# Products of constants put into TensorE's waits in the second block's scan and latent up-projection

## The chip, the cores and the metric

The kernel runs on one core of a Trainium2 chip. The metric is the device time of one execution in microseconds (us); smaller is better. Its engines are named as in the profile: PE (TensorE, matrix products), PEld (its weight loads), DVE (VectorE), ACT (ScalarE), POOL (GpSimd) and SP (SyncE, which issues most DMAs). TensorE's clock has two levels, 1.2 and 2.4 GHz; the profile gives the granted clock as a share of 2.4 GHz, so 0.50 is the lower level and 1.00 the upper.

## The reference

Six transformer layers on 512 tokens of width 1024: four of a first block (two with forgetting attention, one S5, one pooling) and two of a second block, whose mixer is cut here to what the change touches:

```python
def hybrid_mixer(h, ...):
    proj = h @ w_in
    q_a, kv_a, k_pe, z, xbc, dt_raw = split(proj)
    q = (rmsnorm(q_a) @ w_q_up).reshape(b, s, MLA_HEADS, QK_HEAD_DIM)        # 8 heads of 64 + 32
    kv = (rmsnorm(kv_a) @ w_kv_up).reshape(b, s, MLA_HEADS, 64 + 64)
    # q_nope, q_pe, k_nope, k_pe are normalised, the pe parts rotated
    attn_out = causal_attention(q_full, k_full, v)
    # xbc goes through a convolution and silu, and gives xs, bm, cm
    y = ssd_chunked(xs, dt, a, bm, cm) + d_skip * xs                         # 4 chunks of 128 tokens, 8 heads
    yg = rmsnorm(y * silu(z)) * ssd_norm_w
    return concatenate([attn_out, yg]) @ w_out
```

## The kernel before, in words

The program is a list of stages that run one after the other (`plan`). Most stages form a Block of their own; a Block ends when all engines are at its end. Within a stage each engine has its own hand-written order (`tensor`, `scalar`, `gpsimd`, `vector`, `sync`), and engines wait for one another by semaphores (`e.wait_ge`, `then_inc`). TensorE's instructions are issued in the order written, so an instruction that is added stands ahead of everything behind it. SP loads the weights two slots ahead, under `chunk_done`.

A mixer of the second block is the stages `SecondIn`, `Ssd`, `LatentUp`, `LatentAttention` and `SplitProject`; it occurs twice, about 706 us apart.

`Ssd` (from L2488): TensorE multiplies B by C per chunk (L2522), turns B (L2526), x (L2530) and the rows of dt (L2536), and spreads the last row of the cumulated decays (L2540). ACT takes two exponentials of it (L2602, L2604). DVE scales the turned x (L2663, four instructions, semaphore `xdt_ready`; the last of them reads PSUM bank 7) and then scales these by the decays (L2667, three instructions, `xdtd_ready`). With those TensorE makes the states of three chunks (L2548, in banks 2 and 3), and DVE chains them (L2672 to L2676). Then a loop over 8 heads: `spread(h)` (L2560 to L2562, in banks 0/1 or 6/7), two exponentials on ACT (L2610, L2615), products by the cached C B on DVE (L2688) and POOL (L2634), and `out(h)` on TensorE (L2576, L2578). `spread(h + 1)` is issued ahead of `out(h)`. At the end four squares (L2621) are summed by TensorE (L2588), ACT takes two roots (L2624), DVE takes their reciprocals (L2696) and normalises (L2698).

`LatentUp` (from L2708): POOL packs the query weights (L2835, L2836, `packed`). TensorE makes ten raw tiles (L2765, L2770, L2772) and between them sums squares of the earlier ones in bank 6 (L2753, `stats`), and then four products for v (L2781). ACT takes the root (L2814), DVE the reciprocal (L2848), ACT and DVE split it in two (L2819, L2850, `stat_ready`). Then TensorE spreads the 11 statistics (L2800, banks 0 to 3, the next four ahead of DVE) and rotates three tiles (L2793, banks 4 and 5), DVE multiplies (L2872, L2879) and adds (L2855, L2861, L2865), and POOL does the cosines (L2839).

`LatentAttention` (L1978) follows: logits (L2018, L2019), maximum on DVE (L1948), exponential on ACT (L1900), scaling on POOL (L1918), turns on TensorE (L1796) and the product by v (L1809). ACT and DVE also split the first chunk of the output weights there (L1196, L1203).

`keep_warm(bank, n)` (L291) is in the kernel already: n products of two constants, `identb` by `pastb`, 128x512 in bf16, into a bank that nobody reads. All of its instructions have line L294. It is called in the norms, at the end of the projections and in three other stages, but nowhere in `Ssd`, `LatentUp` or `LatentAttention`.

Of the kernel before, what the change touches and what calls it, by code (L numbers as in the profile page):

```python
# [25 lines left out]
ST = S // P  # L26
# [55 lines left out]
def due(n):  # L82

    return not isinstance(n, int) or n > 0
# [248 lines left out]
class Stage:  # L333
    n = 0
# [10 lines left out]
    def tensor(self, e): pass  # L345
# [293 lines left out]
class PoolMix(Stage):  # L639

    n = 1
# [86 lines left out]
class S5Mix(Stage):  # L728


    n = 4
# [897 lines left out]
class FoxV(Split):  # L1629


    n = 4
# [94 lines left out]
class FoxAttention(Split):  # L1727


    n = FH // 2  # L1730
# [247 lines left out]
class LatentAttention(FoxAttention):  # L1978


    n = 0
# [40 lines left out]
class SplitProject(Split):  # L2022


    n = 4
# [191 lines left out]
class SplitGlu(Split):  # L2217


    n = DK  # L2220
# [102 lines left out]
class SecondIn(Split):  # L2323


    n = 8
# [161 lines left out]
class Ssd(Stage):  # L2488
# [24 lines left out]
    def tensor(self, e):  # L2513
        m, nc = self.m, self.m.nc
        ident = m.c("ident")
        tr, mm = nc.tensor.transpose, nc.tensor.matmul
        ps = m.ps

        for g in range(2):
            for c in range(ST):  # L2520
                cs = slice(c * P, (c + 1) * P)
                last = mm(ps[:, g, cs], self.bT(g)[:, cs], self.cT(g)[:, cs], start=True, stop=True)  # L2522
            last.then_inc(m.sem["cb_done"], 1)
        for g in range(2):
            for c in range(ST):
                last = tr(ps[:, 2 + g, c * P:(c + 1) * P], self.bT(g)[:, c * P:(c + 1) * P], ident)  # L2526
            last.then_inc(m.sem["bt_done"], 1)
        for c in range(ST):
            for t in range(4):
                last = tr(ps[:, 4 + c, t * P:(t + 1) * P], self.xs(t)[:, c * P:(c + 1) * P], ident)  # L2530
            last.then_inc(m.sem["xt_done"], 1)
        e.wait_ge(m.sem["acs_ready"], m.at("acs_ready", 1))
        e.wait_ge(m.sem["cb_ready"], m.at("cb_ready", 1))
        for i, src in enumerate((self.dt, self.acs)):
            for c in range(ST):
                last = tr(ps[:, 0, 32 * i + 8 * c:32 * i + 8 * c + 8], src[0:MH, c * P:(c + 1) * P], ident[0:MH, 0:MH])  # L2536
        last.then_inc(m.sem["rows_turned"], 1)
        e.wait_ge(m.sem["acsT_ready"], m.at("acsT_ready", 1))
        e.wait_ge(m.sem["cb_ready"], m.at("cb_ready", 2))
        mm(ps[:, 1, 0:32], m.c("last"), self.acsT, start=True, stop=True).then_inc(m.sem["last_spread"], 1)  # L2540

        for c in range(ST - 1):
            e.wait_ge(m.sem["xdtd_ready"], m.at("xdtd_ready", c + 1))
            e.wait_ge(m.sem["bt_ready2"], m.at("bt_ready2", 2))
            if due(c - 1):
                e.wait_ge(m.sem["st_ready"], m.at("st_ready", c - 1))
            for g in range(2):
                last = mm(ps[:, 2 + c % 2, g * 256:(g + 1) * 256], self.btok[:, g, c, :], self.xdtd[c][:, g * 256:(g + 1) * 256], start=True, stop=True)  # L2548
            last.then_inc(m.sem["st_done"], 1)

        def spread(h):
            b = 6 if h % 2 else 0
            e.wait_ge(m.sem["am_ready"], m.at("am_ready", h + 1))
            if h == 0:
                e.wait_ge(m.sem["decay_ready"], m.at("decay_ready", 1))
            if h == 1:
                e.wait_ge(m.sem["xdt_ready"], m.at("xdt_ready", ST))
            if due(h - 1):
                e.wait_ge(m.sem["l_ready"], m.at("l_ready", h - 1))
            mm(ps[:, b, :], m.ones[0:MH, :], self.am[h % 2][0:MH], start=True, stop=True).then_inc(m.sem["bc_ready"], 1)  # L2560
            mm(ps[:, b + 1, :], m.ones[32:MR, :], self.am[h % 2][32:MR], start=True, stop=False)
            mm(ps[:, b + 1, :], m.identb[:], m.pastb[:].rearrange("p (a n) -> p a n", a=1).broadcast_to([P, ST, P]), start=False, stop=True).then_inc(m.sem["bm_ready"], 1)  # L2562

        def out(h):
            bank = 4 + (h // 2) % 2
            e.wait_ge(m.sem["sc_ready"], m.at("sc_ready", h + 1))
            e.wait_ge(m.sem["cth_ready"], m.at("cth_ready", h + 1))
            e.wait_ge(m.sem["st_ready"], m.at("st_ready", ST - 1))
            if h == 0:
                e.wait_ge(m.sem["xdt_ready"], m.at("xdt_ready", ST))  # L2570
            if due(h // 2 - 1):
                e.wait_ge(m.sem["y_gated"], m.at("y_gated", h // 2 - 1))
            r = 64 * (h % 2)
            for c in range(ST):
                cs, hs = slice(c * P, (c + 1) * P), slice(h * 64, (h + 1) * 64)
                last = mm(ps[r:r + 64, bank, cs], self.xdt[c][:, hs], self.sc[h % 2][:, cs], start=True, stop=c == 0)  # L2576
                if c:
                    last = mm(ps[r:r + 64, bank, cs], self.st[c][:, hs], self.cth[h % 2][:, cs], start=False, stop=True)  # L2578
            last.then_inc(m.sem["yh_done"], 1)

        spread(0)
        for h in range(MH):
            if h + 1 < MH:
                spread(h + 1)
            out(h)
        for t in range(4):
            e.wait_ge(m.sem["ysq_ready"], m.at("ysq_ready", t + 1))
            last = mm(ps[:, 2 + t // 2, :], m.ones[:], m.sq[:, t % 2, :], start=t % 2 == 0, stop=t % 2 == 1)  # L2588
            last.then_inc(m.sem["ysq_used"], 1)

    def scalar(self, e):
        m, nc = self.m, self.m.nc
# [115 lines left out]
class LatentUp(Stage):  # L2708


    n = 2
# [33 lines left out]
    def tensor(self, e):  # L2745
        m, nc = self.m, self.m.nc
        mm, ps = nc.tensor.matmul, m.ps
        nope, pe = (self.packed[:, a:b].rearrange("p (k n) -> p k n", k=2) for a, b in ((0, 1024), (1024, 1536)))
        wk, wv = (m.w[(self.c0 + 1) % 2][:, 512 * i:512 * i + 512] for i in range(2))

        def stats(n):
            e.wait_ge(m.sem["isq_ready"], m.at("isq_ready", n + 1))
            mm(ps[0:32, 6, :], self.gather(n), self.square(n), start=n == 0, stop=n == self.N - 1).then_inc(m.sem["isq_used"], 1)  # L2753

        for n in range(1, self.N):
            if n == 1 or n == 3:
                e.wait_ge(m.sem["packed"], m.at("packed", 1 + n // 3))
            if n == 4:
                self.landed(e, 1, (self.c0 + 1) % 2)
            if n >= 5:  # L2760
                e.wait_ge(m.sem["raw_taken"], m.at("raw_taken", n - 4))
            out = ps[:, n % 4, :]
            if n < 3:
                for k in range(2):
                    last = mm(out, pe[:, k, P * n - P:P * n], m.lat[:, k, :], start=k == 0, stop=k == 1)  # L2765
            else:
                i = (n - 3) // 2
                if n % 2:
                    for k in range(2):
                        last = mm(out, nope[:, k, P * i:P * i + P], m.lat[:, k, :], start=k == 0, stop=k == 1)  # L2770
                else:
                    last = mm(out, wk[:, P * i:P * i + P], m.lat[:, 2, :], start=True, stop=True)  # L2772
            last.then_inc(m.sem["raw_ready"], 1)
            if n >= 3:
                stats(n - 3)
        for n in range(self.N - 3, self.N):
            stats(n)
        for t in range(ST):
            if t >= 2:
                e.wait_ge(m.sem["lv_taken"], m.at("lv_taken", t - 1))  # L2780
            last = mm(ps[:, 4 + t % 2, :], m.lat[:, 2, t * P:(t + 1) * P], wv, start=True, stop=True)  # L2781
            if t < ST - 1:
                last.then_inc(m.sem["lv_done"], 1)
        last.then_inc(m.chunk_done, 2)
        e.wait_ge(m.sem["stat_ready"], m.at("stat_ready", 1))

        def rotate(i):
            e.wait_ge(m.sem["normed"], m.at("normed", i + 1))
            if i == 0:
                e.wait_ge(m.sem["lv_taken"], m.at("lv_taken", ST))  # L2790
            if i == 2:
                e.wait_ge(m.sem["rot_taken"], m.at("rot_taken", 1))
            mm(ps[:, 4 + i % 2, :], m.c("rot"), self.pe[i], start=True, stop=True).then_inc(m.sem["rot_done"], 1)  # L2793

        for n in range(self.N):
            if n < 4:
                e.wait_ge(m.sem["raw_taken"], m.at("raw_taken", self.N - 1))
            else:
                e.wait_ge(m.sem["normed"], m.at("normed", n - 3))
            mm(ps[:, n % 4, :], m.spread[:, n * P:(n + 1) * P], m.stat2[0:64, :], start=True, stop=True).then_inc(m.sem["stat_spread"], 1)  # L2800
            if 3 <= n < 6:
                rotate(n - 3)

    def scalar(self, e):
        m, nc = self.m, self.m.nc
# [289 lines left out]
```

## Time and profile before

| | |
|---|---|
| median of 3 runs | 3875.01 us (3874.47 to 3875.34) |
| the profiled execution's own time | 3879.85 us |
| its span, from first to last instruction | 3878.0 us |
| mean granted TensorE clock | 0.969 |
| PE busy | 3611.3 us, 93% of the span, 16819 products |
| DVE, POOL, ACT busy | 53%, 28%, 28% |
| HBM traffic | 89 GB/s over the span |

The rows come from the profiled execution, so a sum made of them is made against 3879.85 us. Times in a timeline are microseconds from the start of the span; a row merges neighbouring instructions of one line ("x4"), its second number is how long they took in all, and the square bracket is the engine's idle time ahead of it and who ended it.

### The profile page before, as it was taken

The page shows a single profiled execution, that of the slowest core. Times are in us where ns is not written, and L with a number is a line of the kernel's source. Part 1 is how long each engine was busy: PE and PEld are TensorE (multiplying, and loading weights), DVE is VectorE, ACT ScalarE, POOL GpSimd, SP SyncE. Part 2 cuts the span into 40 slices and gives each one's busy share as a digit, 9 for nine tenths or more (in the row PEclk, how much of TensorE's full clock was granted, in tenths as well). Part 3 has the DMA queues.
Part 4 walks back from the last instruction along what each step waited for, and adds up shares of the span by engine and source line. Part 5 has one row for each costly group of instructions (what it writes and reads, how often), then busy time and mean ns, then how long its engine had stood idle before and what let it go on. Part 6 is the DMA issues. An engine that isn't in the chain of part 4 may idle for free. (4 is left out here: it accounts for less than half of the span.)

```text
span 3878.0 us, 44362 instructions
## 1 busy us (share of the span) xinstructions
PE 3611.3 (93%) x16819; PEld 2825.1 (73%) x16819; DVE 2053.9 (53%) x2627; ACT 1078.7 (28%) x1480; POOL 1100.2 (28%) x835
## 2 busy tenths in 40 slices
PE   7999999979999979999899999986899999689999
PEld 6767888757788858887667888762688877267887
DVE  4556556784544475455456545665533356654334
ACT  3542221131312122223452121333322223332121
POOL 0645543700645236340554634012100000130000
PEclk9999999989999989999999999997999999899999
DMA  3215443123444334442214443200133331013332
GB/s 106 61 49 131 128 132 98 52 69 94 136 129 133 90 87 135 126 115 80 66 41 116 131 130 107 80 25 22 55 102 99 87 88 47 22 44 87 92 99 80
DMA packets 554575, 346.08 MB, mean 89 GB/s; under 512 B 33526, under 2 KB 535676, under 8 KB 554428
## 3 DMA queue, kind: packets, MB, share of 16 engines
q1 hardware_dynamic: 540604, 293.80, 27.0%
q0 software_dynamic: 13824, 50.34, 4.5%
q8 instruction: 91, 1.49, 0.2%
q14 instruction: 56, 0.46, 0.0%
HBM read 341.01 MB, written 3.08 MB: 89 GB/s over the span
## 5 line engine op out<-in xcount | busy, mean ns | idle before, releaser
L1241 PE MATMUL ps<-h_hi,w_hi 128*128 128x512 f32 x2880 | 1143.6, 397 | 44.6 <-DVE w_lo L1203 15.3
L1242 PE MATMUL ps<-h_lo,w_hi 128*128 128x512 f32 x2880 | 1126.4, 391 | 0.0
L1243 PE MATMUL ps<-h_hi,w_lo 128*128 128x512 f32 x2880 | 1125.6, 391 | 0.0
L1203 DVE TENSOR_TENSOR w_lo<-w,w_hi 128x2048 fp32r<-128x2048 f32 (+2 forms) x294 | 663.1, 2256 | 138.4 <-ACT w_hi L1196 136.1
L1196 ACT ACTIVATE w_hi<-w 128x2048 fp32r<-128x2048 f32 (+2 forms) x294 | 507.2, 1726 | 713.0 <-PE ps L1243 634.5
L1241 PEld LDWEIGHTS ps<-h_hi,w_hi 128*128 128x128 f32 x2880 | 544.6, 189 | 163.9 <-issue 39.8
L1243 PEld LDWEIGHTS ps<-h_hi,w_lo 128*128 128x128 f32 x2880 | 543.6, 189 | 115.3
L1242 PEld LDWEIGHTS ps<-h_lo,w_hi 128*128 128x128 f32 x2880 | 544.4, 189 | 107.4 <-issue 0.5
L1332 DVE TENSOR_TENSOR sg<-sg,ps 128x512 f32<-128x512 f32 x132 | 90.9, 689 | 718.7 <-ACT sg L1317 718.7
L1241 PE MATMUL ps<-a_hi,w_hi 128*128 128x512 f32 x1056 | 412.4, 391 | 2.6 <-DVE w_lo L1203 2.6
L1243 PE MATMUL ps<-a_hi,w_lo 128*128 128x512 f32 x1056 | 411.0, 389 | 0.0
L1242 PE MATMUL ps<-a_lo,w_hi 128*128 128x512 f32 x1056 | 410.9, 389 | 0.0
L1317 ACT ACTIVATE sg<-ps 128x512 f32<-128x512 f32 x132 | 79.0, 598 | 1088.5 <-PE ps L1243 1088.3
L1114 POOL TENSOR_TENSOR w<-w,cact 128x1024 f32<-128x1024 f32 x96 | 184.8, 1925 | 452.7 <-PE ps L1300 452.4
L1116 POOL TENSOR_TENSOR w<-w 128x512 f32<-128x512 f32 x192 | 241.7, 1259 | 15.1
L1241 PEld LDWEIGHTS ps<-a_hi,w_hi 128*128 128x128 f32 x1056 | 198.3, 188 | 45.1 <-DVE w_lo L1203 4.2
L1243 PEld LDWEIGHTS ps<-a_hi,w_lo 128*128 128x128 f32 x1056 | 198.2, 188 | 41.4
L1242 PEld LDWEIGHTS ps<-a_lo,w_hi 128*128 128x128 f32 x1056 | 198.3, 188 | 40.8
L1105 POOL DMA_DIRECT2D w<-in_w_ada x96 | 88.5, 922 | 419.5 <-POOLq L2990 353.6
L1117 POOL TENSOR_TENSOR w<-w 128x128 f32<-128x128 f32 x96 | 195.0, 2032 | 7.5
L1918 POOL TENSOR_SCALAR misc<-misc,small 128x128 f32<-128x128 f32 (+3 forms) x128 | 165.3, 1297 | 92.9 <-DVE small L1932 91.3
L1948 DVE TENSOR_REDUCE small<-ps 128x1 f32<-128x128 f32 x192 | 93.1, 487 | 158.1 <-PE ps L1787 124.8
(467 smaller groups left out, 3926.0 us busy)
## 6 DMA issues: line engine op xcount, KB each, us to landing
w<-in_ffn_w_gate_up SPq DMA_DIRECT2D x176, 512.0 KB
w<-in_w_ada POOLq DMA_DIRECT2D x96, 512.0 KB, 6.9
w<-in_ffn_w_down SPq DMA_DIRECT2D x64, 704.0 KB
w<-in_w_gate_up SPq DMA_DIRECT2D x88, 512.0 KB
w<-in_w_down SPq DMA_DIRECT2D x32, 704.0 KB
w<-in_fox_w_in SPq DMA_DIRECT2D x32, 512.0 KB
w<-in_w_in SPq DMA_DIRECT2D x14, 1024.0 KB
w<-in_fox_w_in SPq DMA_DIRECT2D x8, 1024.0 KB
```

Of the source, the lines that this page charges most:

```text
L1105: nc.gpsimd.dma_start(three(m.ada_w[:, u % 2, :]), self.source(u)).then_inc(m.sem["ada_in"], 16)
L1114: m.pool(e, tt(three(p), three(m.ada_w[:, u % 2, :]), c, ALU.mult))
L1116: m.pool(e, tt(p[:, 0:n], p[:, 0:n], p[:, n:2 * n], ALU.add))
L1117: tt(p[:, 0:P], p[:, 0:P], p[:, P:2 * P], ALU.add).then_inc(m.sem["ada_summed"], 1)
L1196: last = nc.scalar.activation(hi, raw, ACT.Copy)
L1203: last = nc.vector.tensor_tensor(lo, raw, hi.bitcast(F32), ALU.subtract)
L1241: nc.tensor.matmul(out, hi, a[0][:, k, :], start=k == 0, stop=False)
L1242: nc.tensor.matmul(out, hi, a[1][:, k, :], start=False, stop=False)
L1243: return nc.tensor.matmul(out, lo, a[0][:, k, :], start=False, stop=k == kt - 1)
L1332: m.dve(e, nc.vector.tensor_tensor(t, m.sg[:, par(j), 0, :], m.ps[:, par(j) * 2 + 1, :], ALU.mult))
L1918: nc.gpsimd.tensor_scalar(self.pb[s % 2][t], self.pb[s % 2][t], self.stat(self.ri, s, t), None, ALU.mult).then_inc(m.sem["p_scaled"], 1)
L1948: nc.vector.tensor_reduce(self.stat(self.nm, s, t), m.ps[:, 2 + t % 2, 0:(t + 1) * P], AX.X, ALU.max, negate=True).then_inc(m.sem["max_rea ...
```

## The change

Eight calls of `keep_warm`, all into bank 7, and one wait ahead of the first of them. Nothing is removed. Per mixer 38 products are added in `Ssd` (10 + 4 + 4 + 20) and 72 in `LatentUp` (20 + 12 + five times 2 + 30), so 220 in the kernel, each with its weight load.

```diff
@@ Ssd.tensor
         mm(ps[:, 1, 0:32], m.c("last"), self.acsT, start=True, stop=True).then_inc(m.sem["last_spread"], 1)
-
+        e.wait_ge(m.sem["xdt_ready"], m.at("xdt_ready", ST))
+        m.keep_warm(7, 10)
         for c in range(ST - 1):
             e.wait_ge(m.sem["xdtd_ready"], m.at("xdtd_ready", c + 1))
...
         for t in range(4):
+            if t > 1:
+                m.keep_warm(7, 4)
             e.wait_ge(m.sem["ysq_ready"], m.at("ysq_ready", t + 1))
             last = mm(ps[:, 2 + t // 2, :], m.ones[:], m.sq[:, t % 2, :], start=t % 2 == 0, stop=t % 2 == 1)
             last.then_inc(m.sem["ysq_used"], 1)
+        m.keep_warm(7, 20)
@@ LatentUp.tensor
+        m.keep_warm(7, 20)
         for n in range(1, self.N):
             if n == 1 or n == 3:
                 e.wait_ge(m.sem["packed"], m.at("packed", 1 + n // 3))
...
         last.then_inc(m.chunk_done, 2)
+        m.keep_warm(7, 12)
         e.wait_ge(m.sem["stat_ready"], m.at("stat_ready", 1))
...
             if 3 <= n < 6:
                 rotate(n - 3)
+            if n >= 6:
+                m.keep_warm(7, 2)
+        m.keep_warm(7, 30)
```

## Rows read from the trace of the kernel before

**Rows 1.** The page: engines, and the granted clock in 40 slices of the span.
```profile
PE 3611.3 (93%) x16819; PEld 2825.1 (73%) x16819; DVE 2053.9 (53%) x2627; ACT 1078.7 (28%) x1480; POOL 1100.2 (28%) x835
...
PEclk9999999989999989999999999997999999899999
```

**Rows 2.** Busy time by stretch, both mixers: stretch, length, each engine's busy, PEclk, DMA.
```profile
core 0: us, PE busy (x) PEld busy (x) DVE busy (x) ACT busy (x) POOL busy (x), PEclk, DMA share, GB/s
2571.40:2576.00 4.60, 0.05 (x2) 0.01 (x1) 4.13 (x9) 0.43 (x2) 0.00 (x0) 0.83 0.00 0
2576.00:2581.30 5.30, 5.30 (x12) 3.85 (x12) 3.20 (x5) 0.00 (x0) 0.00 (x0) 0.51 0.00 0
...
2585.00:2588.10 3.10, 3.06 (x14) 2.85 (x14) 2.39 (x3) 0.65 (x3) 1.11 (x1) 0.51 0.01 3
...
2614.10:2622.20 8.10, 0.00 (x0) 0.00 (x0) 6.90 (x6) 1.31 (x2) 0.61 (x2) 0.79 0.00 0
2622.20:2627.40 5.20, 5.15 (x8) 2.27 (x9) 0.69 (x1) 0.61 (x2) 0.97 (x1) 0.67 0.02 3
...
2655.20:2666.40 11.20, 9.92 (x17) 3.57 (x17) 9.80 (x14) 0.17 (x1) 3.81 (x3) 0.70 0.53 177
2666.40:2679.30 12.90, 0.00 (x0) 0.00 (x0) 12.14 (x18) 4.26 (x8) 0.00 (x0) 0.51 0.00 1
...
2684.40:2694.00 9.60, 8.60 (x22) 4.89 (x23) 3.03 (x11) 3.12 (x11) 4.99 (x6) 0.51 0.00 0
...
3328.70:3333.90 5.20, 5.16 (x8) 2.27 (x9) 0.69 (x1) 0.61 (x2) 0.97 (x1) 0.67 0.00 0
```

**Rows 3.** Timeline, the constants' products at the end of a projection.
```profile
3492.63 4.49 PE L294 MATMUL ps<-pastb,identb 128*128 128x512 bf16 x20
```

**Rows 4.** Timeline, the states and first heads of the first scan.
```profile
2572.67 2.47 DVE L2663 TENSOR_TENSOR arena<-ps,small 128x512 f32<-128x512 f32 x4
2575.24 1.90 DVE L2667 TENSOR_TENSOR arena<-arena,small 128x512 f32<-128x512 f32 x3
2575.99 5.43 PE L2548 MATMUL ps<-arena 128*128 128x256 f32 x12 [4.55 <-DVE arena L2667]
...
2585.04 1.12 PE L2576 MATMUL ps<-arena 128*64 128x128 f32 x4 [0.87 <-DVE arena L2688]
...
2589.55 0.65 PE L2576 MATMUL ps<-arena 128*64 128x128 f32 x4
```

**Rows 5.** Timeline, the end of the first scan and the next Block's start.
```profile
2612.09 1.98 PE L2588 MATMUL ps<-sq,ones 128*128 128x512 f32 x4 [1.29 <-ACT sq L2621]
2614.11 0.69 ACT L2624 ACTIVATE arena<-ps,eps 128x512 f32<-128x512 f32 x1 [1.56 <-PE ps L2588]
...
2616.27 3.35 DVE L2696 RECIPROCAL arena<-arena 128x512 f32<-128x512 f32 x1
2619.65 1.41 DVE L2698 SCALAR_TENSOR_TENSOR arena<-arena,cols 128x512 f32<-128x512 f32 x2
...
2621.59 0.61 POOL L2835 COPY arena<-w 128x512 f32<-128x512 f32 x1 [15.05 <-POOLq L2990]
...
2622.25 5.34 PE L2765 MATMUL ps<-lat,arena 128*128 128x512 f32 x8 [8.18 <-POOL arena L2835]
```

**Rows 6.** Timeline, the first products of the two scans, after equal idle times.
```profile
2565.46 2.02 PE L2522 MATMUL ps<-arena 128*128 128x128 f32 x16 [2.75 <-PEq L2990]
...
3270.22 3.30 PE L2522 MATMUL ps<-arena 128*128 128x128 f32 x16 [2.75 <-PEq L2990]
```

**Rows 7.** Timeline, the latent projections up to their last DVE work.
```profile
2632.25 1.98 PE L2770 MATMUL ps<-lat,arena 128*128 128x512 f32 x4
...
2649.59 3.86 PE L2781 MATMUL ps<-w,lat 128*128 128x512 f32 x8
...
2655.18 1.21 PE L2800 MATMUL ps<-stat,spread 64*128 64x512 f32 x4 [1.73 <-DVE stat L2850]
...
2662.15 1.51 DVE L2879 SCALAR_TENSOR_TENSOR arena<-arena,cols,ps 64x512 f32<-64x512 f32 x2 [0.50 <-PE ps L2800]
...
2677.33 1.50 DVE L2879 SCALAR_TENSOR_TENSOR arena<-arena,cols,ps 64x512 f32<-64x512 f32 x2
```

**Rows 8.** Timeline, TensorE early in the first latent attention.
```profile
2679.36 0.77 PE L2018 MATMUL ps<-arena 96*128 96x128 f32 x2 [13.02 <-PEq L2990]
...
2684.44 1.65 PE L2018 MATMUL ps<-arena 96*128 96x384 f32 x2 [3.14 <-ACT arena L1900]
```

## The prediction

> **What bounds the kernel now.** I read the page first. PE is busy 93% of the span and its granted clock is near full in nearly every slice [rows 1], so over the whole kernel there is little to win from a clock; one of the few dips is a slice that falls on the first mixer's stages. Then I cut that mixer into stretches [rows 2]. The reader should look at two columns together, PE busy and PEclk: where PE idles, the clock only matters for what comes after; where PE is busy at 0.51, products take about twice as long, and it is on the path if the others idle. Four such stretches show: the states of the scan (5.30 us busy at 0.51), the first head's output (3.06 at 0.51), the first latent products (5.15 at 0.67) and the start of the attention (8.60 at 0.51). Between 2655.2 and 2666.4 the clock is 0.70 too, but DVE is busy 9.80 of 11.2 us, so it bounds there. The second mixer repeats the first (3328.7, same 0.67) [rows 2], so I cost one and double it. Last I read timelines around each place where products are put in: when TensorE's wait really ends, and whether the added products fit ahead of that end.
>
> **What one added product costs.** Twenty took 4.49 us, which is 19 starts and a tail, so 0.216 us each at full clock [rows 3]; at the lower clock I take twice that, 0.43. An added product that runs past the end of the wait it fills delays all behind it, since TensorE issues in order.
>
> **The ten products before the states.** Their wait is for the fourth L2663, which ends at 2572.67 + 2.47 = 2575.14. The clock is then down: the hole from 2571.4 to 2576.0 has 0.83 and what follows 0.51 [rows 2]. The wait itself comes too late to fill most of that hole. Ten at 0.43 end at 2579.4; the states began at 2575.99, behind the first L2667 [rows 4], so they begin 3.4 us late. They took 12 x 0.44 us; the clock came up at about 2581.2, when they were done. Now four run at 0.44 and eight at an estimated 0.24 and they end at 2583.1 instead of 2581.3: +1.8. What stands behind them is spread(0), and behind that ACT's exponentials, DVE's product and out(0), all waiting for it; nothing covers this. In return, more solid work may keep the clock up for out(0), which now takes 3.1 us at 0.51, four L2576 in 1.12 us against 0.65 for the next head [rows 2, 4]: about -1.5 if it holds. I see no row that decides, and take the middle of +1.8 and +0.3, **+1.1**. Ends: -1.3 (the clock comes up while the constants run, and stays) and +3.4 (the whole delay stays).
>
> **The end of the scan.** Four products in the 1.29 us gap before t = 2 take 0.86 and fit. Four before t = 3 stand behind a square that is then ready, so the last sum and ACT's root at 2614.11 come up to 0.86 us later; the root feeds the reciprocal that DVE starts only at 2616.27 because it is busy until then [rows 5]: root done at 2614.80 + 0.86 = 2615.66, still early, **0**. If DVE were earlier it would cost 0.9. The closing twenty run from 2614.95 to 2619.3, beside DVE, which ends the Block at 2619.65 + 1.41 = 2621.06 [rows 5]: **0**.
>
> **Twenty before the latent products.** This is the largest term. The Block starts at about 2621.6 (POOL's first copy), and TensorE's real wait is only that copy of 0.61 us: its first product starts at 2622.25 [rows 5]. Twenty products do not fit in 0.65 us. At full clock they end at 2621.6 + 4.3 = 2625.9, 3.7 us later than the wait does. What they buy: the first eight passes took 5.2 us at 0.67 and take 8 x 0.49 = 3.9 at full clock, by L2770 [rows 2, 5, 7], -1.3. The net is +2.3 if the clock stays up through the idle 2.3 us between the closing twenty and the new ones. Does it? After an equal idle time of 2.75 us the sixteen L2522 took 2.02 us in the first scan and 3.30 in the second [rows 6], so holes of this length lose the clock sometimes. If it falls, it comes up after a stretch at half speed like the one there is now (0.67 over 5.2 us is 3.4 us at the lower level), which costs another 1.7: **+4.0**. I take this, because the clock fell here in both mixers and at 2.3 us the hole is closer to those that lost it. Twenty wholly at the lower clock would make +6.4, the upper end. From 2622 to 2653 PE has no idle time, so all of it reaches the end: root, reciprocal and split wait for the last L2753.
>
> **Twelve before the statistics.** The products for v end at 2649.59 + 3.86 = 2653.45, and the statistic is there at 2655.18 [rows 7]. Twelve take 2.6 us and end at 2656.05: +0.9. With the clock kept up the rotations and spreads no longer hold DVE. It idles 1.40 us in that part (11.20 less 9.80), some 0.7 of it until its first product is there, and 0.50 in one later place [rows 2, 7], so about 0.7 comes back: **+0.2**, ends -0.2 and +0.9.
>
> **Two per tile, and thirty at the end.** Two take 0.43 us (0.86 at the lower clock) in each turn of DVE, whose two L2879 alone take 1.5 us, and TensorE works four banks ahead: **0**. Thirty start near 2666.8 and take 6.5 us, 12.9 at the lower clock; DVE ends at 2677.33 + 1.50 = 2678.83 [rows 7]: **0**, at most +0.9. They are meant for the attention, but stop about 5 us before it. And the attention has a hole of its own, 3.14 us ahead of L2018 at 2684.44 [rows 8], while the exponential's table and the split of the output weights are waited for. I expect its start at half clock as before, **0**. Were it all at full clock, at most half of its 8.60 busy us would go [rows 2]: -4.3.
>
> The added wait on xdt_ready holds only TensorE, and what is behind it needs a later instruction of the same engine anyway: nothing of its own. No DMA is added or moved; the weights for these stages are there, as the DMA share of 0.00 and the POOL wait show [rows 2, 5].
>
> **Sum.** 1.1 + 4.0 + 0.2 = 5.3 us for each mixer, 10.6 for two. Against the profiled execution that is 3879.85 + 10.6 = 3890.4. That execution is 4.84 us above the median of the runs shown, which I take as the price of profiling, so 3875.01 + 10.6 = **3885.6 us**, 0.27% slower.
>
> **A rule that speaks for the change.** PE is busy at the lower clock for 5.3 + 3.1 + 3.4 + 6.7 + 8.6 = 27.1 us per mixer (5.15 at 0.67 and 11.2 at 0.70 hold 3.4 and 6.7 of it) [rows 2]. The Trainium skill, "TensorE: Matmul & The Clock Gate", Terms, prices throttled time at 1 - K/N of it, half here. The first latent stretch agrees roughly: 3.4 us at the lower level for 1.3 us lost against full-clock passes [rows 2, 5, 7]. But that price holds only where PE is what the others wait for; between 2655.2 and 2666.4 DVE is.
>
> **Rivals.**
> (a) *The clock survives the Block boundary, and the scan gets its out(0) back.* For: one of the two holes of 2.75 us [rows 6]. Against: it was down here in both mixers. Per mixer +2.3 + 0.3 + 0.2 = 2.8, so 3875.0 + 5.6 = 3880.6, 0.14%, under what can be told from no change.
> (b) *Faster: the whole of the lost clock comes back.* The place is every stretch where PE is busy at the lower clock, the attention's start above all. The price is half of 27.1, -13.6, against the products on the path at full clock: 1.3 before the states (2.2 less the 0.85 they gain by starting early), 3.7 and 0.9, in all +5.9. That makes -7.7 per mixer, 3859.6 us. It decides as soon as more than 5.9 us per mixer come back. Against it: the hole before L2018, the thirty that end too soon, the wait that begins after the clock has gone, and DVE's bound.
> (c) *The constants run at the lower clock throughout:* +3.4, +6.4, +0.9 and +0.9 per mixer, 3898.2 us.
>
> **How the numbers follow.** A measurement of this kernel tells about 0.2% from no change, 7.75 us, so slower begins at 3882.8. The forecast with its neighbours, where the clock falls at the boundary in at least one mixer, has 0.58; (c) 0.03; (a), with smaller gains in the scan or the attention that bring the sum under 7.75, 0.33; (b) 0.06. The range takes in (a) and some gain at the attention on the low side, and a full delay before the states on the high side: 3876 to 3891.
>
> **What would show it.** Right: L2765 begins 4 to 6 us after POOL's first copy instead of 0.66, behind twenty L294; L2548 begins over 3 us after the first L2667 instead of 0.75; DVE's last L2879 ends the Block as before, with the thirty L294 done ahead of it; the attention's first stretches still show a clock near 0.5. Wrong: the attention's start at 1.00 and its first heads shorter, or L2765 starting within 1 us of the copy.

## The result, and the profile after

The changed kernel takes 3896.44 us (median of 5 runs, 3890.86 to 3901.34) against 3875.01 us (5 runs, 3874.22 to 3876.80): ratio 1.0052, 95% interval 1.0041 to 1.0062. It is 21.4 us slower, twice the 10.6 us of the forecast and above its range of 3876 to 3891. Its profiled execution has a span of 3899.6 us, 21.6 us more than before. Its five runs span 10 us; those of the kernel before span 3 here, but 6.6 to 9.5 in the larger sets further down, so the spread by itself says little.

First the page of the changed kernel, engines and granted clock in 40 slices.

```profile
PE 3671.3 (94%) x17039; PEld 2845.5 (73%) x17039; DVE 2053.5 (53%) x2627; ACT 1078.7 (28%) x1480; POOL 1100.2 (28%) x835
...
PEclk9999999989999989999999999998999999999999
```

PE has 220 more products and 60 us more busy time, and the dip in the clock by the first mixer is smaller; yet the kernel is slower. "Busier, at a better clock" is no gain by itself.

Now stretches of the changed kernel's first mixer (columns as in [rows 2]).

```profile
2575.20:2579.40 4.20, 4.20 (x10) 1.66 (x11) 1.90 (x3) 0.00 (x0) 0.00 (x0) 0.50 0.00 0
2579.40:2583.20 3.80, 3.79 (x13) 2.64 (x11) 1.62 (x3) 0.00 (x0) 0.00 (x0) 0.76 0.00 0
2587.90:2594.80 6.90, 6.90 (x27) 4.35 (x25) 2.56 (x5) 1.69 (x5) 1.39 (x2) 0.51 0.01 2
2625.20:2631.20 6.00, 5.96 (x20) 2.49 (x21) 0.00 (x0) 0.63 (x1) 1.59 (x2) 0.72 0.00 0
2631.20:2634.70 3.50, 3.50 (x10) 1.56 (x10) 0.69 (x1) 0.60 (x1) 0.00 (x0) 1.00 0.00 0
2678.90:2688.30 9.40, 9.39 (x33) 3.63 (x32) 7.76 (x11) 2.02 (x4) 0.00 (x0) 0.75 0.00 0
2693.60:2703.30 9.70, 8.67 (x22) 4.78 (x23) 3.03 (x11) 3.34 (x13) 5.19 (x6) 0.51 0.00 0
2751.80:2755.30 3.50, 3.15 (x8) 2.51 (x9) 3.50 (x7) 3.50 (x7) 0.00 (x0) 0.51 0.87 294
```

The ten constants run at the lower clock (0.50, ten in 4.20 us). The states behind them get part of the upper one (0.76). Then comes the surprise: the clock is down from 2588 to 2595, where PE is busy for all of 6.90 us with heads of the scan. Before, the heads behind out(0) ran at 1.00 and only the first out(0) was slow, 3.06 us [rows 2]. The last row is the output projection's first chunk, at full clock before and here at 0.51. The same two places in the kernel before (the first row has the columns of [rows 2]; the second is of PE alone: length, busy, clock, DMA):

```profile
2588.10:2614.10 26.00, 24.09 (x137) 14.23 (x136) 15.36 (x19) 13.83 (x36) 8.39 (x6) 1.00 0.00 1
2735.00:2760.00 25.00, 21.20 (x103) 1.00 0.24 85
```

The timeline around each place, to be read beside [rows 4, 5, 7, 8]:

```profile
2575.19 4.45 PE L294 MATMUL ps<-pastb,identb 128*128 128x512 bf16 x10 [3.76 <-DVE arena L2667]
2579.43 3.89 PE L2549 MATMUL ps<-arena 128*128 128x256 f32 x12
...
2586.95 0.65 PE L2577 MATMUL ps<-arena 128*64 128x128 f32 x4 [0.87 <-DVE arena L2692]
...
2591.67 1.12 PE L2577 MATMUL ps<-arena 128*64 128x128 f32 x4
...
2625.22 0.61 POOL L2844 COPY arena<-w 128x512 f32<-128x512 f32 x1 [15.05 <-POOLq L2999]
2625.24 6.16 PE L294 MATMUL ps<-pastb,identb 128*128 128x512 bf16 x20 [2.35 <-PEq L2999]
...
2631.24 3.60 PE L2770 MATMUL ps<-lat,arena 128*128 128x512 f32 x8
...
2660.52 2.75 PE L294 MATMUL ps<-pastb,identb 128*128 128x512 bf16 x12
...
2663.21 1.21 PE L2806 MATMUL ps<-stat,spread 64*128 64x512 f32 x4
...
2678.91 9.38 PE L294 MATMUL ps<-pastb,identb 128*128 128x512 bf16 x32
...
2685.31 1.50 DVE L2888 SCALAR_TENSOR_TENSOR arena<-arena,cols,ps 64x512 f32<-64x512 f32 x2
...
2688.59 0.46 PE L2018 MATMUL ps<-arena 96*128 96x128 f32 x2 [0.30 <-PEq L2999]
...
2693.67 1.52 PE L2018 MATMUL ps<-arena 96*128 96x384 f32 x2 [4.02 <-ACT arena L1900]
```

(L2549 is L2548 of before, L2577 is L2576, L2770 is L2765, L2806 is L2800, L2888 is L2879.) Out(0) now has the upper clock, out(1) has lost it. The first latent product starts 6.0 us behind POOL's copy. The last thirty end at 2688.29, 1.5 us after DVE's last work at 2686.81, and the attention has to wait for them.

DVE runs the same instructions in the same order in both kernels, so the difference between their starts, taken at a few of them, says where time is lost (called the DVE reading below). Its change from one to the next, in us:

| step | forecast, per mixer | first mixer | second mixer |
|---|---|---|---|
| ten, up to the end of the states | 1.8 | +1.9 | +1.6 |
| heads of the scan | -1.5 to 0 (together 1.1) | +1.7 | +1.7 |
| end of the scan | 0 | 0 | 0 |
| twenty, first latent products | 4.0 | +3.6 | +3.6 |
| twelve, and DVE's part behind it | 0.2 | +0.8 | +1.0 |
| thirty | 0 | +1.25 | +1.0 |
| attention, first heads | 0 | +0.4 | +0.3 |
| projection's first chunk | 0 | +1.5 | +1.4 |
| sum | 5.3 | 11.15 | 10.6 |

The two sums exceed the span's 21.6 by 0.2 us, which were gained between the mixers. Two kinds of loss were not in the forecast: the heads of the scan, and places where nothing was put in.

### The profile page after: what moved, and what is told of

It is laid out like the page before. It is cut to its first block and busy times, and to the rows that moved or that the text cites. A ratio compares the mean times of both kernels' runs of the same rounds, so it can differ in the third digit from the quotient of the medians.

```text
span 3899.6 us, 44802 instructions
## 1 busy us (share of the span) xinstructions
PE 3671.3 (94%) x17039; PEld 2845.5 (73%) x17039; DVE 2053.5 (53%) x2627; ACT 1078.7 (28%) x1480; POOL 1100.2 (28%) x835
```

## The experiments

Two theories. **Order:** a constants' product costs the time by which it outlasts the wait it stands in, and nothing else. **Clock:** what it also does is move the stretches at the lower clock, and those cost wherever PE is the bound, even outside the changed stages. First the change in four pieces, then kernels that tell the two apart. The kernel of before ran beside each; +us is the difference of medians. The steps read from a trace need not sum to it: a trace is one execution, and that of before is itself late. At 2501 us, ahead of everything that was changed, it is 2.5 to 6.1 us behind every other trace but the changed kernel's.

**a_ten_only.**

```diff
+        e.wait_ge(m.sem["xdt_ready"], m.at("xdt_ready", ST))
+        m.keep_warm(7, 10)
         for c in range(ST - 1):
```

> Only the wait and the ten products before the states, in both mixers. Order theory (products cost only the time by which they outlast the wait they fill): the first spread starts 1.4 to 1.9 us later in each mixer and nothing more, about +3.5 us against before. Clock theory (the delay also moves the stretches at the lower clock onto busier ones): another 1.7 us per mixer between the first spread and the squares, as in the changed kernel's trace, about +7 us. If the two places downstream that were also slower in the changed kernel (first heads of the attention, output projection) only need a shifted start, up to +10.

3886.01 against 3877.34, ratio 1.0023 (1.0011 to 1.0035). But the eleven runs are not one group: five from 3876.7 to 3880.8, one at 3886.0, five from 3893.9 to 3896.3. The median is the one run between the groups, so its +8.7 us is typical of neither. The profiled one is of the upper group. Its stretches from the statistics to the attention's first heads, and from the attention's end into the projection:

```profile
2655.00:2696.00 41.00, 23.80 (x51) 10.85 (x50) 28.43 (x46) 11.41 (x24) 9.62 (x9) 0.51 0.14 46
2737.40:2751.00 13.60, 10.13 (x29) 6.22 (x30) 7.40 (x12) 6.53 (x10) 0.00 (x0) 0.50 0.24 77
```

By the same DVE reading, each mixer loses 1.7 in the states, 1.7 in the heads, 0.6 in the statistics, 0.7 in the attention's start, 2.2 at the attention's end and 2.6 in the projection. More than half is lost behind the scan, where this kernel is the same as before. Order alone (+3.5) is refuted for this execution (3895.61 us); the clock theory's +10 was still too small.

**b_scan_end_only.**

```diff
+            if t > 1:
+                m.keep_warm(7, 4)
...
+        m.keep_warm(7, 20)
```

> Only four + four + twenty at the end of the scan. Order theory: 0, they lie beside DVE's reciprocals and normalisation. Clock theory: -2.6 to 0, since a clock that is kept up to the Block's end could be up for part of the first latent products; a positive time over 1 us speaks against both.

3876.52, ratio 0.9999 (0.9990 to 1.0008): nothing, which both theories allow.

**c_twenty_start_only.**

```diff
+        m.keep_warm(7, 20)
         for n in range(1, self.N):
```

> Only the twenty before the latent products. Order theory as in the prediction: L2770 starts 5.4 us later (the hole before them is longer here, so the clock is down at their start) and 1.4 us of it come back, +4.0 per mixer, about +8 us. Nothing should be lost elsewhere by this theory; the clock theory adds up to 3 us downstream (output projection).

3892.82, ratio 1.0040 (1.0027 to 1.0053), +15.5 us. The place itself takes 3.9 us per mixer, as forecast. The rest is again elsewhere: per mixer 0.6 in the statistics, 0.8 at the attention's start, 2.2 at its end and 2.6 in the projection, and 3.0 in the heads of the first mixer. The trace is of the slowest of the five runs (3898.59 us). Its 3.0 stands ahead of the first product that was added, where the kernel is still that of before: the clock alone can cost this much in one execution, so a step read from one trace is firm only where it comes back in both mixers or in other traces. At the attention's end:

```profile
2738.78 1.31 PE L1796 MATMUL ps<-consts,arena 128*128 128x128 f32 x10 [1.88 <-DVE arena L1885]
2741.20 4.53 PE L1809 MATMUL ps<-arena 128*64 128x512 f32 x16 [1.11 <-DVE arena L1885]
2748.27 0.77 PE L1241 MATMUL ps<-h_hi,w_hi 128*128 128x512 f32 x1 [2.54 <-DVE h_lo L2064]
```

The same place in the kernel before:

```profile
2735.15 1.30 PE L1796 MATMUL ps<-consts,arena 128*128 128x128 f32 x10 [1.88 <-DVE arena L1885]
2737.56 2.37 PE L1809 MATMUL ps<-arena 128*64 128x512 f32 x16 [1.11 <-DVE arena L1885]
```

Idle times 1.88 and 1.11 are equal to a hundredth; only the product by v behind them takes 4.53 us instead of 2.37. That is the clock, not an order or a wait: it was 1.00 here from 2731 to 2740, and 0.50 from 2740.1 to 2753.7.

**d_latent_end_only.**

```diff
+        m.keep_warm(7, 12)
         e.wait_ge(m.sem["stat_ready"], m.at("stat_ready", 1))
...
+            if n >= 6:
+                m.keep_warm(7, 2)
+        m.keep_warm(7, 30)
```

> Only the twelve, the twos and the thirty of the latent stage. The changed kernel's trace gives +0.8 per mixer for the twelve and +1.1 for the thirty outlasting DVE's last work, so +3.8 us by the order theory. The prediction had +0.4 for all of them. If this part also causes the slower first heads and projection, +3.7 more, about +7.5.

3875.82, ratio 0.9997 (0.9988 to 1.0006). The twelve cost 0.8 in both mixers, and DVE's part and the attention's start give 0.6 back. The thirty cost nothing here, where they start at 2668.5, behind the last twos: they outlast DVE only if they begin late enough or at the lower clock, as in the changed kernel.

**c2_twenty_and_fill.** The fill puts products into short waits, none longer than its wait:

```diff
@@ the attention's tensor; self.n == 0 holds for LatentAttention alone
+        if self.n == 0:
+            self.m.keep_warm(0, 7)
         for t in range(ST):
             self.turn(e, self.heads - 1, t)
+        if self.n == 0:
+            self.m.keep_warm(0, 4)
         self.times_v(e, self.heads // 2 - 1)
+        if self.n == 0:
+            self.m.keep_warm(0, 3)
...
@@ SplitProject.tensor; self.gate is set in the second block alone
+        if self.gate:
+            m.keep_warm(6, 6)
```

> The twenty before the latent products, as in c_twenty_start_only (+15.5 us), and constants' products in the three short waits at the end of the latent attention and the start of the output projection, none longer than its wait. Theory: about half of the +15.5 is the order (+3.6 to +4.0 per mixer) and the rest is the clock being down from the attention's last head into the projection (in that run's trace the work between 2727 and 2750 lost 4.7 us more). If so the fill takes the second part away: +8 us against before. Rival, that the twenty cost all of it where they stand: still +15.

3884.83 against 3875.64, ratio 1.0027 (1.0017 to 1.0036), +9.2 us instead of +15.5. The stretch that had 0.50 above:

```profile
2655.80:2696.80 41.00, 23.85 (x51) 10.91 (x50) 28.56 (x47) 11.40 (x24) 9.63 (x9) 0.50 0.13 44
2738.90:2752.50 13.60, 13.23 (x63) 8.98 (x64) 7.89 (x10) 6.08 (x9) 0.00 (x0) 1.00 0.27 85
```

With the clock at 1.00 there, the DVE reading shows 0.00 at the attention's end and 0.00 in the projection; what stays is 3.9 for the twenty, 0.65 in the statistics and 0.75 at the attention's start, some 5.3 per mixer. The first row, still 0.50, shows that the fill touched nothing ahead of it.

**i_fill_only.** The fill by itself.

> Only the fill at the attention's end, the control for the three kernels that hold it. In most traces of before the clock is up there anyway, so 0 within 0.2%; the spread of the runs may become smaller.

3875.69 against 3876.26, ratio 0.9999 (0.9990 to 1.0008). So the fill by itself gains nothing, and what it takes off c_twenty_start_only is a loss prevented, not one made up for.

**a2_ten_and_fill.** The ten and the fill.

> The ten before the states (eleven runs of them alone fell in two groups, near 3879 and near 3895) with the fill at the attention's end. Theory: the upper group is the clock being down from the attention's end into the projection, which the fill prevents, so one group remains, +5 to +8 over before, and no run near 3895. Rival: two groups remain.

3879.92 against 3876.26, ratio 1.0009 (0.9999 to 1.0018), +3.7 us and not clear of no change; eleven runs from 3876.8 to 3883.7. The upper group is gone. The median is below what was expected, because the ten do not always cost the same: 1.8 + 1.8 in the first mixer of this trace, but 0.2 and -0.1 in the second, where the clock came up while the constants ran.

**f_all_but_twenty.**

> The whole change without the twenty before the latent products. If the parts add up, the changed kernel's +21 loses what the order theory gives for the twenty (7.2 us in its own trace): +14. If the clock's place downstream is what matters, it may come out anywhere from +3 (the ten alone, lower group of runs) to +19.

3885.34, ratio 1.0029 (1.0016 to 1.0041), +9.7 us (six runs). The trace has 1.8 + 1.7 for the ten and 0.8 for the twelve in both mixers; the attention's end and the projection lost 3.3 us in the first mixer and nothing in the second. The change without the twenty is some 12 us faster than with it, where the twenty's own 7.2 would be the order's share; the ranges of the two (3880.7 to 3894.4 and 3890.9 to 3901.3) overlap, so the 12 is rough.

**after_and_fill.** The whole change and the fill.

> The whole change with the fill at the attention's end. The changed kernel's trace loses 1.5 us per mixer in the projection's first chunk: theory, that goes (-3 us against the changed kernel), and the runs that lost more there go too, leaving the sum of the places in the mixers, 3.4 + 3.6 + 0.8 + 1.2 + 0.4 per mixer, +17 to +19 against before.

3890.32 against 3876.26, ratio 1.0041 (1.0027 to 1.0054), +14.1 us, range 3884.2 to 3897.2. The fill takes some 7 us off the changed kernel's +21.4, more than the 3 expected and within the spread of either. Its profiled run is the lowest of its five; there the ten cost 0.25 and the projection 0, and the twenty and twelve 3.5 and 0.8, as in the changed kernel's trace.

**e_wait_only.** The added wait without products.

> Only the added wait on xdt_ready, no products. Both theories: what is behind it on TensorE needs a later DVE instruction anyway, so 0, within 0.2%. A rival in which the wait itself costs: L2548 starting later than 0.75 us after the first L2667.

3876.52 against 3875.64, ratio 1.0001 (0.9992 to 1.0010): the wait is free, and the products are what costs.

**j_seventeen_early.** The same purpose as the ten, from the beginning of the hole and in a bank that is free there:

```diff
         mm(ps[:, 1, 0:32], m.c("last"), self.acsT, start=True, stop=True).then_inc(m.sem["last_spread"], 1)
+        m.keep_warm(0, 17)
```

> Only seventeen products in bank 0 directly behind L2540, without the added wait: they end before DVE's first L2667 would release the states. Theory: the states run at full clock, -2.4 per mixer, and the first head's output may keep it, -1.5 more: -4 to -8 us against before, as the trace of h_sized has it. Rival: the clock falls one step later, as with the ten, and the gain is taken back: 0.

3869.18 against 3876.26, ratio 0.9983 (0.9974 to 0.9992), 7.1 us faster; nine of the eleven runs lie from 3867.4 to 3870.8, the other two at 3874.1 and 3876.4.

```profile
2566.66 0.41 PE L2540 MATMUL ps<-small,consts 128*128 128x32 f32 x2 [0.32 <-DVE small L2647]
2566.90 3.83 PE L294 MATMUL ps<-pastb,identb 128*128 128x512 bf16 x17
2571.61 3.11 PE L2548 MATMUL ps<-arena 128*128 128x256 f32 x12 [0.88 <-DVE arena L2667]
...
2578.35 0.65 PE L2576 MATMUL ps<-arena 128*64 128x128 f32 x4 [0.87 <-DVE arena L2688]
```

The seventeen end 0.9 us before the states are released, these take 3.11 us instead of 5.43 [rows 4], and out(0) has the upper clock: -2.3 and -1.5 per mixer. The rival (a loss one step later) did not come in this trace; whether it did in the two slower runs is open.

**h_sized.** Every group sized to end inside its wait. Here as the difference from the changed kernel, put together, with remarks on the place:

```diff
-        m.keep_warm(7, 10)        # and the wait; before the states
+        m.keep_warm(0, 17)        # right behind L2540
-            if t > 1:
+            if t == 2:
                 m.keep_warm(7, 4)
-        m.keep_warm(7, 20)        # end of the scan
+        m.keep_warm(7, 27)
-        m.keep_warm(7, 20)        # before the latent products
+        m.keep_warm(7, 2)
-        m.keep_warm(7, 12)        # before the statistics
+        m.keep_warm(7, 7)
-            if n >= 6:
-                m.keep_warm(7, 2)
-        m.keep_warm(7, 30)        # end of the latent stage
+        m.keep_warm(7, 45)
+        if i == 2:                # in the attention's hole, before its third logits
+            m.keep_warm(0, 13)
```

and the fill.

> Constants' products sized so that each group ends before its wait does: 17 in bank 0 right behind L2540 (no added wait) in place of the ten, 4 before t = 2 only, 27 at the scan's end, 2 before the latent products, 7 before the statistics, 45 at the latent stage's end, 13 in the attention's hole before its third logits, and the fill at the attention's end. Clock theory: the states (-2.4 per mixer), the first head's output (-1.5), the latent products (-1.3) and the attention's start (-1 to -2.9) come back: -12 to -16 us against before. Rival, that nothing but the placement of delays matters and clocks come back elsewhere as losses: 0 or slower.

3859.77 against 3875.64, ratio 0.9954 (0.9940 to 0.9968): 15.9 us faster than before and some 37 faster than the changed kernel. The attention's start:

```profile
2669.60 0.46 PE L2026 MATMUL ps<-arena 96*128 96x128 f32 x2 [0.56 <-PEq L3006]
...
2670.50 2.97 PE L294 MATMUL ps<-pastb,identb 128*128 128x512 bf16 x13
2674.68 0.91 PE L2026 MATMUL ps<-arena 96*128 96x384 f32 x2 [1.21 <-ACT arena L1906]
```

The logits behind the hole take 0.91 us instead of 1.65 [rows 8], and the attention's first heads give 3.7 us per mixer. States and heads give 3.8 in the first mixer, the latent products 1.6 in each. One loss stays: +2.7 in the heads of the second mixer.

## Why the prediction was wrong

- *The ten: "+1.8", right; "In return, more solid work may keep the clock up for out(0)", wrong.* Out(0) got the upper clock, but the lower one came right behind it, over 6.90 us in which PE had no idle time, and took 1.7 more. I had placed the end of the clock's effect at the first head. The term was 1.1; with the heads it measured 3.6 and 3.3 in this trace (0.1 in the second mixer of a2_ten_and_fill, where the clock came up under the constants). This is the step that failed most: 4.7 of the 11.1 us by which the steps of the trace exceed the 10.6.
- *"The end of the scan: 0"*: right, and b_scan_end_only shows it alone.
- *The twenty: "+4.0"*: right, 3.6 with the rest of the change and 3.9 alone. The clock did fall at the Block's boundary, though not in the hole: it was 1.00 over all of its 2.3 us and fell 0.3 us into the twenty (0.72 over them). The eight passes took 3.60 us instead of 5.34 [rows 5], so full clock gave back 1.7 and not 1.3.
- *The twelve: "+0.2"*: the 0.8 is there in every trace. What was to come back from DVE came back in d_latent_end_only (0.4), but not in the changed kernel: the clock fell in the middle of the rotations.
- *"Thirty ... 0, at most +0.9"*: 1.25 and 1.0. They began 12 us later than the 2666.8 taken, at 2678.91 with the last twos. 7 to 8 us of that are the delays ahead, which DVE shares; against DVE they began 4 to 5 us late, and the 32 products took 9.38 us, at 0.75. I had not carried the other terms' side effects (twos at the lower clock held PE back) into this one's start.
- *"The added wait ... nothing of its own"*: right, e_wait_only.
- *The attention: "its start at half clock as before, 0"*: right for the clock (0.51), +0.4 for its length. The gain that I bounded by 4.3 exists: 3.7 with the hole filled (h_sized).
- *No term at all for the attention's end and the projection.* They lost 1.5 and 1.4 us in the changed kernel, 4.8 per mixer in the traces of a_ten_only and c_twenty_start_only, and nothing once the short waits there were filled. The sum ended with the stages that the diff touches, and this is the other step that failed.
- *Rival (b)*, that the lost clock comes back, was wrong for this change and right as a price: h_sized collects it, 3859.8 us against the 3859.6 worked out for it, though by other means (each group inside its wait) and so partly by chance.
- *Rival (c)*, every constant at the lower clock, has the number that came nearest, 3898.2 against 3896.4, and that is luck. Only the ten ran so (0.50); the twenty had 0.72 and cost 3.6 instead of 6.4, the twelve ran at full clock (2.75 us), and the heads and the projection, with 6.3 us over both mixers, are not in it.
- *"4.84 us ... the price of profiling"*: wrong as a reading. The profiled executions of b_scan_end_only, d_latent_end_only, e_wait_only, i_fill_only and j_seventeen_early are within 1.3 us of their medians; that of before had run late ahead of the changed stages. The forecast hangs on the median and is not touched by it.
- *The signs:* L2770 (L2765 of before) began 6.0 us behind POOL's copy, and the states 4.2 us behind DVE's first product for them, as said; the attention began at 0.51, as said. But the thirty, not DVE, ended the Block.
- *The rule on throttled time.* The Trainium skill ("TensorE: Matmul & The Clock Gate", Terms) puts the loss at half of the throttled time at this ratio. The traces agree where PE is the bound: the final product by v lost 2.16 of 4.53 us at the lower clock, the states 2.3 of 5.4.

What stays open: why the clock's fall lands on one stretch or the next from run to run (a_ten_only in two groups, c_twenty_start_only in one heads' part), and with it how much of the +21.4 is typical of a given run. The first products of the two scans show the same chance: behind 2.75 us of idle time in every trace, the sixteen L2522 took 2.02 us in some and 3.02 to 3.64 in others. That the parts add up to the whole was not shown exactly: the pieces' differences (8.7, -0.8, 15.5, -1.5) sum to about the same, but two of them hold the same kind of downstream loss.

## What to carry to other kernels

In these runs, products put in to hold the clock paid when they started with the idle time and ended before the wait did: seventeen at the beginning of a hole won 7 us where ten at its end, behind an added wait, lost 8.7 at the median, or 3.7 with the short waits downstream filled. Count it at the clock that is granted at that moment, and behind an in-order engine price the first real instruction, not the wait. Then follow the clock's row beyond the changed stages: a delay of a few microseconds can put the lower clock onto short waits that were harmless before, and filling those is cheap insurance.

## What the runs showed of the hardware that I had not expected

- TensorE lost its upper clock in the middle of work: in the changed kernel it fell at about 2588, in the second microsecond of out(0). Ahead of it stood the states, 2.8 us mostly of spreads, products with only 8 rows (L2561, L2562), and one hole of 0.87 us, the only one since 2579. PE was busy 7.71 of the 8.60 us before the fall, so its busy column did not announce it; what in this stretch brought the fall was not tried.
- The clock can stay down for long over half-busy work: 41 us at 0.51 with PE busy 23.8 of them (a_ten_only), where before it was up for a part of that time (0.70 from 2655.2 to 2666.4 [rows 2]).
- Two waits of 1.88 and 1.11 us, the same to a hundredth in both kernels, stood ahead of a product by v at the upper clock in one (2.37 us) and at the lower in the other (4.53 us, c_twenty_start_only).
